# A decoder block on one core: branch c's gates behind the latent projections, both attentions behind the recurrence's levels

## The reference

```python
h = rms_norm(x, attn_norm)
proj = h @ w_in          # queries, keys, values, latents and 3 x 1024 gate logits
o_a = dsa_attention(...)  # 4 heads; 64 best keys by an index score; softmax with a position bias
o_b = hgrn2_mixer(...)    # gated linear recurrence, then rms_norm and silu(g)
q_c = rms_norm(cq, mla_q_norm) @ mla_w_qb      # latent queries
kv_c = rms_norm(ckv, mla_kv_norm) @ mla_w_kvb  # latent keys and values
o_c = mla_attention(...)  # 4 heads, with rope on a part of queries and keys
mixed = g_a * (o_a @ w_up_a) + g_b * (o_b @ w_up_b) + g_c * (o_c @ w_up_c)
x = x + mixed @ w_out
x = x + (silu(h2 @ w_ffn_gate) * (h2 @ w_ffn_up)) @ w_ffn_down
```

## Time and profile before

| | |
|---|---|
| median of 3 runs | 1048.18 us (1047.95 to 1049.42) |
| profiled execution | 1047.96 us, its span 1046.2 us |
| TensorE busy | 1037.4 us, 99% |
| VectorE busy | 734.0 us, 70% |
| ScalarE busy | 581.3 us, 56% |

### The profile page before, as it was taken

The page is one execution under the profiler, slowest core; times in us unless marked ns, Lnnn a source line. Parts: engine busy times, 40 slices in busy tenths (PEclk is TensorE's granted clock), DMA queues, the critical chain, the costliest instruction groups (busy, mean ns, idle before and its releaser), DMA issues.

```text
span 1046.2 us, 22213 instructions
## 1 busy us (share of the span) xinstructions
PE 1037.4 (99%) x8760; PEld 1010.5 (97%) x8760; DVE 734.0 (70%) x1092; ACT 581.3 (56%) x885; POOL 79.3 (8%) x92
## 2 busy tenths in 40 slices
PE   9999999999999999999999999999999999999998
PEld 7999998999999999999999999898899999999998
DVE  6899998647866666657666567567977866665666
ACT  4556655576565554556554445455666665454554
POOL 0000000002310000111000001041001300000110
PEclk9999999999999999999999999999999999999999
DMA  6456533245555554665655456564335555554563
GB/s 220 148 182 215 196 103 133 97 158 197 173 197 200 200 195 138 207 200 190 218 186 194 155 192 218 181 205 174 127 122 202 193 189 185 197 210 147 195 222 121
DMA packets 32444, 187.81 MB, mean 180 GB/s; under 512 B 3832, under 2 KB 7552, under 8 KB 14720
## 3 DMA queue, kind: packets, MB, share of 16 engines
q1 hardware_dynamic: 31472, 185.58, 51.0%
q0 software_dynamic: 416, 1.06, 0.4%
q10 hardware_dynamic: 496, 0.33, 0.1%
HBM read 184.98 MB, written 1.06 MB: 178 GB/s over the span
## 4 chain that ended last, share of the span: by engine, by line
PE 87%; DVE 7%; issue 1%; ACT 0%; DVEq 0%
PE acc L685 83%; PE area_a L685 2%; DVE wlo L1581 2%; PE area_t L685 2%; DVE score L1808 1%; PE area_t L952 1%; DVE work L1821 0%; DVE st L1819 0%; DVE mask L1783 0%; DVE h L1980 0%; DVE s_sum L2138 0%; DVE st L1768 0%; DVE he L1876 0%; DVE he L1877 0%; DVE pp L1617 0%
## 5 line engine op out<-in xcount | busy, mean ns | idle before, releaser
L685 PE MATMUL acc<-hs,whi 128*128 128x256 f32 x3584 | 617.8, 278 | 1.7 <-DVE wlo L1581 1.2
L685 PEld LDWEIGHTS acc<-hs,whi 128*128 128x128 f32 x3584 | 539.3, 187 | 8.5 <-issue 4.6
L685 PE MATMUL acc<-hs,wlo 128*128 128x256 f32 x1792 | 495.0, 276 | 0.0
L1184 ACT ACTIVATE whi<-raw 128x1024 fp32r<-128x1024 f32 (+3 forms) x379 | 357.0, 978 | 169.0 <-PE acc L685 151.2
L1581 DVE TENSOR_TENSOR wlo<-raw,whi 128x1024 fp32r<-128x1024 f32 (+4 forms) x259 | 273.8, 1098 | 99.5 <-ACT whi L1184 98.3
L685 PEld LDWEIGHTS acc<-hs,wlo 128*128 128x128 f32 x1792 | 335.6, 187 | 0.2
L685 PE MATMUL acc<-hid,whi 128*128 128x256 f32 x1056 | 179.7, 276 | 0.0
L685 PEld LDWEIGHTS acc<-hid,whi 128*128 128x128 f32 x1056 | 158.9, 188 | 0.0
L685 PE MATMUL acc<-hid,wlo 128*128 128x256 f32 x528 | 145.7, 276 | 0.0
L1669 DVE TENSOR_TENSOR wlo<-raw,whi 128x1024 fp32r<-128x1024 f32 x120 | 141.1, 1218 | 4.1 <-ACT whi L1184 4.1
L1682 DVE TENSOR_TENSOR hbuf<-acc,sbuf 128x256 f32<-128x256 f32 x66 | 28.0, 425 | 116.8 <-PE acc L685 112.3
(11 more groups left out here) (314 smaller groups left out, 1022.2 us busy)
## 6 DMA issues: line engine op xcount, KB each, us to landing
raw<-in_w_gu SPq DMA_DIRECT2D x66, 1024.0 KB, 4.7
raw<-in_w_dn SPq DMA_DIRECT2D x48, 704.0 KB, 4.1
raw<-in_w_up SPq DMA_DIRECT2D x10, 1024.0 KB, 4.8
raw<-in_w_gates1b SPq DMA_DIRECT2D x8, 1024.0 KB, 4.9
raw<-in_w_out SPq DMA_DIRECT2D x8, 1024.0 KB, 4.8
raw<-in_w_qk SPq DMA_DIRECT2D x8, 1024.0 KB, 4.8
raw<-in_w_gates SPq DMA_DIRECT2D x8, 1024.0 KB, 4.8
raw<-in_w_projT_b SPq DMA_DIRECT2D x7, 1024.0 KB, 4.8
```

Of the source, the lines that this page charges most:

```text
L685: return nc.tensor.matmul(out, w, m, start=start, stop=stop, skip_group_check=True)
L1184: return nc.scalar.activation(out, in_, f, **kw)
```

## The change

The order of tiles is changed: the first four tiles of `w_gates1b` (the gates of branch b) stay behind `w_gates1a` and come before the latent queries `w_qb` and the latent keys and values `w_kvb`; the other four (branch c, now called `gates1c`) come behind them. Before, `w_qb` and `w_kvb` were tiles 21 to 23 and the gates 24 to 31; now the gates are 21 to 24, the latents 25 to 27 and the gates 28 to 31. `rope_k` goes from line 12 to line 8, and the selection of the second half of the queries moves one to two lines back. The levels of the recurrence run one per tile in lines 16 to 23, with no attention among them; both attentions follow in lines 24 to 35, with `hgrn_o` to `hgrn_h` among them. The exponentials get steps of their own (`dsa_e0`, `mla_e0`, `mla_e1`). One load of a table set in `hgrn_n` goes. Buffers get other offsets; their sizes stay.

```diff
     add("w_gates1a", 4, full, full // 2)
+    add("w_gates1b", 4, full, full // 2)
     add("w_qb", 2, 9 * P, 6 * P)
     add("w_kvb", 1, full, full // 2)
-    add("w_gates1b", 8, full, full // 2)
+    tiles.extend(("w_gates1b", i, full, full // 2) for i in range(4, 8))
...
             ("gates1a", 8, lambda i: g["w_gates1a"] + i // 2),
+            ("gates1b", 8, lambda i: g["w_gates1b"] + i // 2),
             ("q_c", 6, lambda i: g["w_qb"] + i // 3), ("kv_c", 6, lambda i: g["w_kvb"]),
-            ("gates1b", 16, lambda i: g["w_gates1b"] + i // 2), ("up1", 24, lambda i: g["w_up1"] + i // 4),
+            ("gates1c", 8, lambda i: g["w_kvb"] + 1 + i // 2), ("up1", 24, lambda i: g["w_up1"] + i // 4),
...
-    work("8a 8b input_squares top_b1 H10 L10")
-    work("9a 9b top_c1 H11 L11")
-    work("10a 10b top_d1 decay_a mla_norm H12 L12")
+    work("8a 8b rope_k H10 L10")
+    work("9a 9b input_squares top_b1 H11 L11")
+    work("10a 10b decay_a mla_norm top_c1 H12 L12")
-    work("12a 12b rope_k H14 L14 decay_xa decay_b")
-    work("13a 13b H15 L15 decay_u")
+    work("12a 12b H14 L14 decay_xa top_d1")
+    work("13a 13b H15 L15 decay_b decay_u")
...
-    work("18a 18b level_x3 level_m3 dsa_s0 lev2 level_e4 H20 L20")
-    work("19a 19b level_x4 level_m4 lev3 dsa_p0 H21 L21")
-    work("20a 20b level_e5 dsa_t0 H22 L22 level_x5 dsa_s1 level_m5 lev4")
-    work("21a 21b H23 L23 level_e6")
-    work("22a 22b dsa_e1 rope_q dsa_p1 level_x6 level_m6")
-    work("23a lev5 H24 L24 23b dsa_t1 level_e7 level_x7 level_m7 H25 L25")
-    work("24a dsa_o 24b mla_s0 lev6 H26 L26")
-    work("25a 25b level_e8 mla_p0 H27 L27")
-    work("26a 26b level_x8 mla_t0 mla_s1 level_m8 mla_p1 H28 L28")
-    work("27a 27b gate_sigmoid1_0 lev7 far H29 L29")
-    work("28a 28b hgrn_o hgrn_gate mla_t1 H30 L30")
-    work("29a 29b hgrn_n H31 L31")
-    work("30a 30b hgrn_v mla_o H32 L32")
-    work("31a 31b H33 L33")
-    work("32a 32b hgrn_h H34 L34")
-    work("33a 33b gate_sigmoid1_1 H35 L35")
-    work("34a 34b gate_sigmoid1_2 H36 L36")
+    work("18a 18b level_x3 level_m3 lev2 level_e4 H20 L20")
+    work("19a 19b level_x4 level_m4 lev3 level_e5 H21 L21")
+    work("20a 20b level_x5 level_m5 lev4 level_e6 H22 L22")
+    work("21a 21b level_x6 level_m6 lev5 level_e7 H23 L23")
+    work("22a 22b level_x7 level_m7 lev6 level_e8 H24 L24")
+    work("23a 23b level_x8 level_m8 lev7 far H25 L25")
+    work("24a dsa_s0 24b H26 dsa_e0 L26 dsa_p0")
+    work("25a 25b H27 L27 dsa_s1")
+    work("26a dsa_t0 26b H28 L28")
+    work("27a rope_q dsa_e1 27b dsa_p1 H29 L29")
+    work("28a mla_s0 dsa_t1 28b H30 mla_e0 L30 mla_p0")
+    work("29a hgrn_o mla_t0 29b H31 hgrn_n L31")
+    work("30a dsa_o 30b H32 mla_s1 L32")
+    work("31a mla_e1 31b H33 gate_sigmoid1_0 mla_p1 L33")
+    work("32a mla_t1 32b H34 hgrn_gate hgrn_v L34")
+    work("33a hgrn_h 33b H35 gate_sigmoid1_1 mla_o L35")
+    work("34a 34b H36 gate_sigmoid1_2 L36")
...
-        d_sc = arena("d_sc", 2048, (4, T))
-        d_p = arena("d_p", 3072, (4, T))
-        d_pt0 = arena("d_pt0", 4096, (4, T))
-        d_pt1 = arena("d_pt1", 5120, (4, P))
+        d_sc = arena("d_sc", 23824, (4, T))
+        d_p = arena("d_p", 22800, (4, T))
+        d_pt0 = arena("d_pt0", 6656, (4, T))
+        d_pt1 = arena("d_pt1", 7680, (4, P))
-        m_sc = arena("m_sc", 8192, (4, T))
-        m_p = arena("m_p", 9216, (4, T))
+        m_sc = arena("m_sc", 23824, (4, T))
+        m_p = arena("m_p", 22800, (4, T))
-        qpe = arena("qpe", 13312, (2, T))
+        qpe = arena("qpe", 21520, (2, T))
-        mixed1 = arena("mixed1", 12288, (KD, T))
-        up1 = arena("up1", 14336, (4, T))
+        mixed1 = arena("mixed1", 16656, (KD, T))
+        up1 = arena("up1", 18704, (4, T))
-        score = arena("score", 26896, (T,))
-        work = arena("work", 27152, (T,))
-        above = arena("above", 27408, (T,))
-        equal = arena("equal", 27664, (T,))
-        rank = arena("rank", 27920, (T,))
+        score = arena("score", 9472, (T,))
+        work = arena("work", 9728, (T,))
+        above = arena("above", 9984, (T,))
+        equal = arena("equal", 11776, (T,))
+        rank = arena("rank", 12032, (T,))
...
                 elif name == "rope_k":
+                    pe.wait_ge(S("con_loaded"), 16)
                     pe.wait_ge(S("keys_doubled"), 32)
...
-        dest("gates1b", [gates[:, k, :] for k in range(8, 24)])
+        dest("gates1b", [gates[:, k, :] for k in range(8, 16)])
+        dest("gates1c", [gates[:, k, :] for k in range(16, 24)])
...
-                elif name in ("dsa_s0", "dsa_e1"):
+                elif name.startswith("dsa_e"):
...
-                elif name.startswith("mla_s"):
+                elif name.startswith("mla_e"):
...
                 elif name == "hgrn_n":
-                    load_set(EXP_AND_LN)
...
-                    last = (("gates1a", 7), ("gates1b", 7), ("gates1b", 15))[b] if first_block else \
+                    last = (("gates1a", 7), ("gates1b", 7), ("gates1c", 7))[b] if first_block else \
```

More of the change, by code:

```diff
@@ L601, in build @@
         BY_SCALAR = {BLOCKS[b] + k for b, c in (("kik", 1), ("iq", 4), ("projT_b", 14), ("bq", 4), ("bg", 4),
-                                                ("gates1a", 8), ("q_c", 6), ("kv_c", 4), ("gates1b", 16))
+                                                ("gates1a", 8), ("gates1b", 8), ("q_c", 6), ("kv_c", 4), ("gates1c", 8))
                      for k in range(c)}
@@ L777, in tile @@
                             "w_gates1a": (BLOCKS["gates1a"], 2),
-                            "w_gates1b": (BLOCKS["gates1b"], 2), "w_out1": (BLOCKS["out1"], 2),
+                            "w_gates1b": (BLOCKS["gates1b"] if i < 4 else BLOCKS["gates1c"] - 8, 2), "w_out1": (BLOCKS["out1"], 2),
                             "w_qk2": (BLOCKS["qk2"], 2), "w_gates2": (BLOCKS["gates2"], 2),
```

## The result

The changed kernel takes 1052.32 us (median of 6 runs, 1052.23 to 1052.59) against 1048.17 us before: ratio 1.0038, 95% interval 1.0026 to 1.0051. It is slower by 4.15 us; forecast were 3.0, and the range (1049.0 to 1053.2) holds the time. The profiled execution has a span of 1050.6 us against 1046.2.

A forecast was written before the change was run, and what follows sets the result against it. TensorE was taken to bound the kernel, so only its idle time could move: −2.55 − 0.15 + 1.1 + 1.4 + 3.2 = +3.0 us on 1048.18, giving 1051.2 us, with a range of 1049.0 to 1053.2.

The forecast's parts named there:

- What bounds it: Whole kernel: TensorE, busy 1037.4 of 1046.2 us at top clock; time can move only by its idle time.
- Removed, 2.55 in the levels: Between 150 and 182 us: four TensorE waits go once attention leaves the levels, 2.55 us less.
- Removed, 0.15 at 81 us: Wait at 81.14 us goes as `rope_k` moves; bounds 0 and 0.42 us, 0.15 taken.
- 1, `far`, 1.1: Line 23: `far` waits for `level_m8`, now in the same line, with only `lev7` to fill; adds 1.1 us.
- 2, `dsa_o`, 1.4: Line 30: `dsa_o` waits for area_a, freed by `hgrn_n` after ScalarE's split of tile 31; adds 1.4 us.
- 3 and 4, the chain through `hgrn_gate`, 1.9 + 1.3: Tile 34 waits for `hgrn_split`, 1.9 us; tile 35 for the PSUM bank of tile 34's first block, 1.3 us.
- a longer load: Rival: each table-set switch stops ScalarE as long again, chain through `hgrn_gate` 2.6 us longer, 1053.8 us; chance 0.05.
- nothing more is lost: From tile 36 on: its split is a tile ahead, and the two kernels are the same work; 0 us added.
- the places that just fit: `mla_s1`, tile 33's first block, `mla_t0`, `dsa_t1`: 0.3 to 1.2 us to spare; 0 to 1 us more, 0 taken.
- The shorter chain: Rival: chain through `hgrn_gate` shorter, last branches' waits partly hidden; 1048.0 to 1049.6 us; chance 0.20.
- the hidden waits: Rival: low halves and products reach TensorE in time at all four late places; 1045.5 us; chance 0.08.
- VectorE as the bound of the levels: Rival: merges and products run longer, stretching each of seven tiles; +7, with the rest 1058 us; chance 0.05.

The follow-up runs named there:

- experiment 7: Changed kernel with lines 8 to 13 of the order as in the kernel before (`rope_k` in line 12 again): 1052.40 us.
- experiment 2: Changed kernel with `far` behind the first half of tile 24 and `dsa_s0` behind the split of tile 26: 1052.23 us.
- experiment 1: Changed kernel with `hgrn_gate` in line 23, `hgrn_v` and `hgrn_h` in line 30, the second sigmoid in line 32: 1048.74 us.
- experiment 4: Changed kernel with one more, unused load of a table set directly before the load of `hgrn_gate`: 1053.66 us.
- Experiment 9: Kernel of experiment 1 with `mla_o` half a tile earlier, in line 33a instead of behind 33b: 1048.17 us.
- experiment 6: Kernel before with only the buffers `mixed1` and `up1` moved to their homes in the changed kernel: 1048.10 us.
- experiment 3: Changed kernel with `hgrn_n` ahead of ScalarE's split of tile 31: 1051.78 us.
- experiment 8: Kernel of experiment 1 with `dsa_o` ahead of `hgrn_o`, `mla_s1` a line earlier, and both sigmoids behind tile 34's high parts: 1056.72 us.
- experiment 12: Changed kernel with the edits of experiments 1, 2, 3 and 9, plus `hgrn_o` half a tile earlier and `hgrn_n` in line 29a ahead of `mla_t0`: 1049.49 us.
- experiment 11: Kernel of experiment 8 with the first sigmoid back in line 31, the second in line 32 and `mla_o` in line 33a: 1051.18 us.

## Why the prediction came out as it did

**What bounds it.** Right. Matmuls, busy time and clock stayed, and the time moved by TensorE's idle time alone.

**Removed, 2.55 in the levels.** Right in mechanism and about right in size: no wait of TensorE in lines 17 to 22, a level with its tile takes 7.25 us where the forecast had 7.24, and some 2.7 came back. No run removes the four one by one; the 2.7 is what is left when the new waits are taken off.

**Removed, 0.15 at 81 us.** Mis-sized: 0. The step named both the bound and the reason (`level_m0` comes no earlier) and then chose above it. The wait of 0.41 in front of level 0, and experiment 7 with the wait back at 81 us and the same time, say that the bound was the answer.

**1, `far`, 1.1.** Measured 1.13, or 1.23 by starts. But experiment 2 got back 0.1 for it at most, not 1.1: the step priced the wait rightly and did not ask what comes behind it. Without that wait VectorE takes nearly all of it back within 27 us.

**2, `dsa_o`, 1.4.** Measured 1.59; the releaser as named.

**3 and 4, the chain through `hgrn_gate`, 1.9 + 1.3.** Measured 1.95 + 1.35, link by link as in the text; experiment 1 takes both away with one move and gets 3.54 back between the same starts. The links were summed from rows of before, and the loads at 1.28 without a drain: experiment 4 bears that out (+1.27 in the wait for one more). The prediction's prices for a longer load take two loads in the chain of 3 and 4. Three stand in it, as the chain above shows, so its own rival would have come to 1051.2 + 3 × 1.28 = 1055.0, not 1053.8.

**The missed term, 0.54 around tile 38.** "Behind it tile 36 finds its split a tile ahead; nothing more is lost, and from half a tile later the two kernels are the same work" failed. The work is the same, its times are not: `mla_o` had gone from line 30 to line 33, its split on VectorE pushed GpSimd's adds onto VectorE's splits, and three tiles later tile 38 started late. Experiment 9 shows it, experiment 6 rules out the buffers' homes by themselves.

**The sum.** 0.15 (a gain that did not come) − 0.15 (the old waits gave back more) + 0.7 (the four losses, 6.4 for 5.7) + 0.54 (missed) = 1.24, on top of 3.0: 4.24. No error is large. The range held the time with room that was left for something else: it went up to 5.0 for the places that just fit, and none of those cost anything in the changed kernel.

**The rivals.** The shorter chain and the hidden waits did not come. A longer load is out. VectorE as the bound of the levels did not come as told (no tile stretched between lines 17 and 22), but in experiment 2 it bounds the stretch right behind them.

## What to carry to other kernels

In a kernel whose main engine is 99% busy, price an order by following each wait to the last instruction that releases it, and then ask who is late next if that wait is gone: here one chain's waits of 3.3 us were worth 3.5 when they were removed, and another wait of 1.1 was worth 0.1 at most. When a short operation is moved into a stretch whose engines step in turn, look whether it makes two of them overlap that did not before. Put an operation early or late by the next user of its PSUM area: three attempts to move the last wait (experiments 3, 8 and 12) made it shorter, gave it to another user or set up a larger one. When an agreement with a theory rests on the median alone, add up the trace: in experiment 4 the time was right and two of its three terms were not in the theory.

## What the runs showed of the hardware

- While TensorE stood still for 3.06 us (experiment 4) the granted clock fell to 0.50, and it was at the top again from 258 us on, some 6 us after work had started; during 5.90 us (experiment 8) it fell as well. In experiment 4 this cost 1.39 us more than the wait that it covered. After 2.38 and 2.50 us (the profiled executions of experiments 12 and 11) it stayed at 1.00, but other runs of the same two kernels read 0.998 in the mean and took over a microsecond longer: whether it falls may differ from one execution to the next.
- The eight matmuls of `far` took 0.91 us to the next start behind a wait (174.67) and 0.81 without one (207.10, before), so this wait cost 0.1 more than its idle time and the record's overhang.
- Two splits of VectorE took 2.4 us alone and 2.9 to 3.4 beside GpSimd's adds; four of those adds 2.84 and 3.8.
- A load of a table set took 1.28 us, two in a row 2.57, with the next activation 0.02 us behind.
